# A hybrid decoder layer: the table of attention biases by distance written to memory 128 times over, and read forwards

## The reference

```python
h    = rmsnorm(x, norm_pre_mix)
proj = h @ w_in            # columns: HGRN2 q f i g, attention q k v, indexer iq ik iw
y_a  = hgrn2_mixer(...)    # gated linear recurrence, 4 heads of 128, log f = log(lb + (1-lb) sigmoid(f))
y_b  = dsa_mixer(...)      # 8 heads of 64; an indexer score picks the top 128 keys of each query
x    = x + rmsnorm(concat(y_a, y_b) @ w_o, norm_post_mix)
h    = rmsnorm(x, norm_pre_ffn)
x    = x + rmsnorm((silu(h @ w_gate) * (h @ w_up)) @ w_down, norm_post_ffn)
# inside dsa_mixer, for query t, key s, head a:
dist   = t - s
logits = q . k * DH ** -0.5 + rel_bias[t5_bucket(dist), a]      # dist < 0 is masked
```

## Time and profile before

| | |
|---|---|
| median of 3 runs | 761.83 us (761.42 to 762.09) |
| profiled execution, own time | 761.42 us |
| its span | 759.6 us |
| mean granted TensorE clock | 0.981 |
| TensorE busy | 713.6 us, 94% of the span |
| VectorE busy | 411.1 us, 54% |
| ScalarE busy | 268.1 us, 35% |
| GpSimd busy | 119.4 us, 16% |
| moved by DMA | 67.03 MB, mean 88 GB/s |

### The profile page before, as it was taken

The page is one execution under the profiler, slowest core; times in us unless marked ns, Lnnn a source line. Parts: engine busy times, 40 slices in busy tenths (PEclk is TensorE's granted clock), DMA queues, the critical chain, the costliest instruction groups (busy, mean ns, idle before and its releaser), DMA issues.

```text
span 759.6 us, 9083 instructions
## 1 busy us (share of the span) xinstructions
PE 713.6 (94%) x3744; PEld 607.5 (80%) x3744; DVE 411.1 (54%) x582; ACT 268.1 (35%) x374; POOL 119.4 (16%) x127
## 2 busy tenths in 40 slices
PE   4889999888999997999999999999999999999996
PEld 2867779888989776898889888888888888888885
DVE  3574898878894997743566234334442443122125
ACT  5354544223352836633444213221332232112112
POOL 4400215444120314730210000000000000000001
PEclk9899999999999998999999999999999999999999
DMA  7223113111145031034222232233223322331302
GB/s 253 73 67 101 56 55 112 56 57 56 32 127 174 28 98 44 1 113 141 81 84 75 93 110 89 79 110 111 86 81 111 111 83 84 111 110 56 111 0 110
DMA packets 49496, 67.03 MB, mean 88 GB/s; under 512 B 3592, under 2 KB 42504, under 8 KB 49456
## 3 DMA queue, kind: packets, MB, share of 16 engines
q1 hardware_dynamic: 46512, 60.59, 25.0%
q0 software_dynamic: 1648, 5.77, 2.2%
q10 hardware_dynamic: 1296, 0.11, 0.1%
HBM read 64.35 MB, written 2.12 MB: 87 GB/s over the span
## 4 chain that ended last, share of the span: by engine, by line
PE 74%; DVE 18%; ACT 3%; issue 2%; DMA 1%; POOL 1%; DVEq 0%; SPq 0%; ACTq 0%
PE PS L935 63%; PE PS L1002 4%; DVE w_lo L637 3%; DVE A L679 2%; DVE top L678 2%; DVE QK L746 2%; PE PS L1096 2%; DVE A L764 1%; DVE A L763 1%; PE PS L1027 1%; DMA A<-in_x_dram 1%; PE PS L974 1%; PE PS L1105 1%; DVE A L787 1%; PE PS L975 1%
## 5 line engine op out<-in xcount | busy, mean ns | idle before, releaser
L935 PE MATMUL PS<-hT_lo,w_hi 128*128 128x512 f32 (+2 forms) x584 | 220.8, 378 | 9.3 <-DVE w_lo L637 7.6
L637 DVE TENSOR_TENSOR w_lo<-raw,w_hi 128x2048 fp32r<-128x2048 f32 (+1 forms) x52 | 125.9, 2422 | 174.7 <-ACT w_hi L447 174.5
L935 PE MATMUL PS<-hT_hi,w_lo 128*128 128x512 f32 (+2 forms) x584 | 219.8, 376 | 0.0
L935 PE MATMUL PS<-hT_hi,w_hi 128*128 128x512 f32 (+2 forms) x584 | 219.7, 376 | 0.0
L447 ACT ACTIVATE w_hi<-raw 128x2048 fp32r<-128x2048 f32 (+1 forms) x52 | 98.2, 1889 | 208.0 <-PE PS L935 207.9
L935 PEld LDWEIGHTS PS<-hT_lo,w_hi 128*128 128x128 f32 (+1 forms) x584 | 112.0, 192 | 30.0 <-DVE w_lo L637 6.5
L935 PEld LDWEIGHTS PS<-hT_hi,w_hi 128*128 128x128 f32 (+1 forms) x584 | 112.0, 192 | 19.7
L935 PEld LDWEIGHTS PS<-hT_hi,w_lo 128*128 128x128 f32 (+1 forms) x584 | 111.9, 192 | 18.8
L935 PE MATMUL PS<-w_hi,ff 128*128 128x512 f32 x352 | 110.7, 395 | 0.0
L355 POOL TENSOR_SCALAR ms<-ss 128x1 f32<-128x1 f32 (+1 forms) x17 | 7.8, 460 | 456.4 <-ACT raw L621 360.6
L935 PEld LDWEIGHTS PS<-w_hi,ff 128*128 128x128 f32 x352 | 66.1, 188 | 15.4
(11 more groups left out here) (152 smaller groups left out, 836.3 us busy)
## 6 DMA issues: line engine op xcount, KB each, us to landing
raw<-in_w_in_dram SPq DMA_DIRECT2D x16, 1024.0 KB, 5.6
raw<-in_w_gate_dram SPq DMA_DIRECT2D x11, 1024.0 KB, 5.3
raw<-in_w_up_dram SPq DMA_DIRECT2D x11, 1024.0 KB, 5.3
raw<-in_w_down_dram SPq DMA_DIRECT2D x11, 1024.0 KB, 4.9
raw<-in_w_o_dram SPq DMA_DIRECT2D x4, 1024.0 KB, 4.9
A<-in_x_dram SPq DMA_DIRECT2D x4, 512.0 KB, 7.9
A<-bias_by_distance POOLq DMA_DIRECT2D x8, 256.0 KB, 4.7
A<-in_x_dram POOLq DMA_DIRECT2D x4, 512.0 KB, 5.3
```

What stands on the lines that cost most here:

```text
L637: dve.tensor_tensor(lo, view(raw[:, j % 2, :], j), hi.bitcast(F32), ALU.subtract).then_inc(s_lo, 1)
L935: o = pe.matmul(out, lhs[a], rhs[b], start=(first and n == 0), stop=(last and n == 2))
```

## The change

The table of distances is turned round (index i now stands for distance 511 - i), the DRAM tensor is made 128 times as large, one copy of a head's 640 values for each partition, and the store from `g_sb` repeats each of its 8 rows 128 times. The loads read, for partition p, from copy p, beginning at value 127 - p, and GpSimd's addition reads a forward slice of `Bh`.

```diff
 def bucket_onehot(seq):
-    n = np.maximum(np.arange(seq + P) - P, 0)
+    n = np.maximum(seq - 1 - np.arange(seq + P), 0)
...
-    gscr = nc.dram_tensor("bias_by_distance", [HEADS_B, S + P], F32, kind="Internal").ap()
+    gscr = nc.dram_tensor("bias_by_distance", [HEADS_B, P, S + P], F32, kind="Internal").ap()
...
             for h in range(HEADS_B):
-                pool.dma_start(Bh[:, h, :], bass.AP(tensor=gscr.tensor, offset=h * (S + P) + 1,
-                                                    ap=[[1, P], [1, S]])).then_inc(s_bh, 16)
+                pool.dma_start(Bh[:, h, :], bass.AP(tensor=gscr.tensor, offset=h * P * (S + P) + P - 1,
+                                                    ap=[[S + P - 1, P], [1, S]])).then_inc(s_bh, 16)
...
-                pool.tensor_tensor(BM[u % 3][:, 0:n], Bh[:, h, 0:n][:, ::-1], M, ALU.add).then_inc(s_bm, 1)
+                pool.tensor_tensor(BM[u % 3][:, 0:n], Bh[:, h, (TB - 1 - b) * P:S], M, ALU.add).then_inc(s_bm, 1)
...
-            act.dma_start(gscr, g_sb).then_inc(s_gst, 16)
+            act.dma_start(gscr, g_sb.unsqueeze(1).to_broadcast([HEADS_B, P, S + P])).then_inc(s_gst, 16)
```

## The result

The changed kernel takes 788.4 us (787.94 to 789.59, 4 runs) against 761.62 us (761.26 to 762.09), a ratio of 1.0354 (1.034 to 1.0368): 26.8 us slower. The forecast was 780 us in a range of 764 to 788. The direction was right, and so was the mechanism in the main. The size was not: 26.0 us in the trace where 18.7 were forecast, and the time is just above the range. The profiled execution took 787.94 us, its span is 785.9.

A forecast was written before the change was run, and what follows sets the result against it. TensorE, with 74% of the chain of waits, was taken to bound the kernel. The store delaying chunk 3 gave 761.4 + 18.7 = 780.1, called 780 us, all other terms 0; range 764 to 788.

The forecast's parts named there:

- Where to look: Before the first `f` matmul TensorE already waits for chunk 3's rounding; anything delaying chunk 3 moves all that follows.
- Each of 8 engines gets 128 rows; the source gives one after another: At the store: repeated rows stay on their row's engine, while eight neighbouring partitions give up rows one after another.
- 45.4 us for the store: Store from `g_sb`: 2,621,440 bytes at 58 GB/s, read from spaced landings, 0.355 us for each row of an engine.
- estimate of 48 us by the Trainium skill: Store: partitions 0 to 7 on two DMA ports of some 27 GB/s each; the sum would end about 3 us higher.
- Some 6 store rows went before chunk 2, so 122 turns are left: On the store's engines: chunk 3, queued behind chunk 2, ends about 0.3 us behind the store, there at 69.1.
- One to one by rows: On shared DMA engines queues take turns row by row, each chunk row waiting for a store row of 0.355 us.
- From the landing to the matmul 4.27 us: After chunk 3 lands at 69.1: rounding 1.92, subtraction 2.30 and 0.05 to the matmul, at 73.4 instead of 54.68.
- Chunk 4, the sigmoid's wait, the loads, the additions: Chunk 4's landing, the first `f` sigmoid's wait on the store, bias loads and GpSimd's additions: 0 each.
- The clock: TensorE's clock after a gap of 18 us starts from the same low level as before: 0 more.
- The rivals with a short row: Store row at 0.13 us: no loss, 761.4 to 762 us, chance 0.15; at 0.25 us: 767 us, chance 0.11.
- slip through: Rival: chunks 2 and 3 land in time, only the first `f` sigmoid waits on the store: 766 to 767 us, chance 0.12.
- reading of 41 GB/s: Rival on the store's rate: store ends near 87 with the chunk rows, 798 us, chance 0.05.

The follow-up runs named there:

- 12 apart: Changed kernel with the store's 8 source partitions 12 apart instead of side by side, against the kernel before on the same chip: 760.57 us, ratio 1.0006.
- the run with eight DMAs: Changed kernel's store split into 8 DMAs of 16 copies each, against the kernel before on the same chip: 778.96 us, ratio 1.0252.

## Why the prediction was wrong

By its own steps:

- *Where to look*: right. Chunk 3 ahead of the `f` group is where the time went, and the rest of the kernel shifted rigidly.
- *Each of 8 engines gets 128 rows; the source gives one after another*: right for the eight engines (47% of 16). For the source it was right in effect, as moving it shows, though 50 GB/s are two ways and not one: 12 apart each partition gave 23 GB/s.
- *45.4 us for the store* (58 GB/s, with the chunk rows 45.4 to 51.8): **this term was too small**. It is the step that put the time outside the range. The store ran from 21.1 to 74.0 us, 53 us, at 50 GB/s, with chunk rows beside it or without (19.5 and 19 rows a microsecond). Seven landings in 0.31 us were read as a rate, but two of the seven came in the same instant as the first and took no time of their own; the five behind them gave 41 GB/s, too little. The first row also landed 1.4 us behind the issue instead of 0.8. The store ended at 74.0 instead of 68.8: 5.2 of the missing 7.3 us. The estimate of 48 us by the Trainium skill ("SBUF — State Buffer", "Door 1: The DMA port swizzle") had the cause right and fell short by 9%.
- *"Some 6 store rows went before chunk 2, so 122 turns are left"*: **this step failed**. About 38 of each engine went before it, some 35 of them after the load had arrived. So each slow engine still had some 38 rows of chunk 3 to move when the store was over. Chunk 3 was done not 0.3 us behind the store but 2.4: 2.1 us. Chunk 2 landed at 64.9 instead of 45 to 48. That cost nothing, but only because 5.9 us were left at ScalarE before chunk 3.
- *One to one by rows*: right in every run with a long store, once the head start is over, except for chunk 2 in the run with eight DMAs. In the changed kernel each of ten stretches of 0.41 us (the time of one store row) from 50.0 us on has 7 or 8 rows of either queue.
- *From the landing to the matmul 4.27 us*: 4.28. *Chunk 4, the sigmoid's wait, the loads, the additions*: nothing, as said. *The clock*: back at 1.00 from 85 us, 4 us after the restart at 80.67, as before.
- The rivals with a short row are refuted: 0.41 us, not 0.13 or 0.25. The loads did not slip through.
- *The range*: its upper end rested on the middle of the store's term. The reading of 41 GB/s stood in the prediction as a rival with 0.05, and 798 us; the truth lay halfway between it and the value taken, where the range should have reached to.

## What to carry to other kernels

A broadcast in a DMA is free in code only: multiply the time of one row by the rows of one engine, and ask how many ways lead out of the source's partitions, before trusting the mean bandwidth. A slow transfer that nobody waits for still delays every load that shares its engines, by its backlog and then by one row for each row, so lay it beside the tightest cover of such a load. If a table must be repeated from on-chip memory, spread the source over the partitions first; here that took a loss of 27 to 30 us to nothing. And before a difference of 1 to 2 us between two traces is given a cause, compare the granted clock in code that both share.

## What was not expected of the hardware

The same 8 rows, repeated on 8 engines, left at 50, 94 or 183 GB/s by their partitions alone. A load that meets a long store on the same engines stood still for 15 us (35 to 38 rows of 2560 bytes) before the first of its rows moved. One DMA of 128 rows an engine was handed over in 1.28 us, but a third DMA behind two of 16 rows took 4.7 us (the second 0.29), and a second one behind one of 128 half rows 6.98 us, and the issuing engine was held. Between profiled executions the same 108 us of code took 1.6 us more where the granted clock was 0.95 instead of 0.97. What the engine's backlog is made of stays open.
